# Five block-product groups per column pair in the down product, weight sums in another order, and the last gain row loaded in four pieces

## The chip, the cores and the metric

One Trainium2 chip, one core. The metric is the device time in microseconds (us); lower is better. The kernel before takes 2435.97 us, the median of three runs (2435.7 to 2436.27).

## The reference, cut to what matters

The reference is a three-layer block on 256 tokens of width 2048, in float32. The change sits in three of its linear layers, and in the last norm:

```
out = (mixed * scale * silu(g)) @ pool_w_out        # 4096 -> 2048, "pool_out"
out = (o * silu(g)) @ mla_w_out                     # 2048 -> 2048, "mla_out"
h   = h + y @ w_down                                # 5504 -> 2048, "down"
out = rms_norm(h, norm_final)                       # h * rsqrt(mean(h*h) + eps) * gain
```

`y` is the 256 x 5504 result of the gated up product. Its 5504 columns are 43 tiles of 128.

## The kernel before, in words

**Products.** A float32 product is made of three matmuls on split operands: high part times high part, high times low, low times high. Weights come from HBM in units of two 128-row tiles by 512 columns (512 KB) into a ring of 8 slots, `raw`. ScalarE writes the high part of a unit into `w_hi` (L1613, L1790), VectorE writes the low part, `w_lo = raw - w_hi` (L2443, L2451), both into rings of 4 slots, and TensorE multiplies (L963 to L965 in the layers of this change). A whole unit costs TensorE 2 tiles x 2 token halves x 3 = 12 matmuls of 512 columns. ScalarE may refill a slot once TensorE has used it (`w_used`), VectorE follows ScalarE (`w_hi`), TensorE follows VectorE (`w_lo`), and SyncE reloads a `raw` slot when the last low part that reads it is written.

**Groups.** Output columns are handled in pairs of 512-column chunks (0 and 1, then 2 and 3). For some of the tiles, a group of four units (two pairs of row tiles by two chunks, the blocks B11, B12, B21, B22) and the two token halves are multiplied with seven block products in place of eight, after Strassen. Each block product is 6 matmuls, so a group costs 42 matmuls where four whole units cost 48. In exchange the weights of a group need four sums on VectorE (L2465, L2467, L2469, L2473) and seven splits on each of ScalarE and VectorE in place of four. The sums of `y` that the groups use are made before the first group: `y_sum` (L2484 to L2492), then their high parts on ScalarE (L2365) and low parts on VectorE (L3447). Four extra PSUM banks hold what a group's blocks share; `quads_out` (L3510 to L3525) reads them into `h` once a pair's last group is done: nine VectorE instructions of 512 columns.

**Order.** `DOWN` writes out by hand the order of whole units and groups of the down product. A pair has 4 groups (tiles 24 to 39) and 14 whole units per chunk (tiles 0 to 23, 40 and 41, and tile 42 alone). In the first pair each group follows four whole units. ScalarE and VectorE walk through the same list, and after certain steps of it do other work: the high and low parts of `y` (`DOWN_Y_STEPS`, L2370 and L3450), `quads_out`, adding finished chunks into `h` (`columns_out`, L2501), squares of `h` on ScalarE (`square_out`, L1647).

**The end.** The last four whole units of chunk 3 are multiplied first for token half 0, then for half 1 (`turned_ending`). GpSimd multiplies chunks 1, 0 and 2 of `h` by the gain of the last norm (L3671), each after ScalarE has squared it. The gain row is one DMA of 1024 KB (L3589, behind the up product). VectorE waits for all three multiplications (L3551), then adds chunk 3 for half 0 (L3555), takes the reciprocal root (L3570), scales (L3573, L3575), adds chunk 3 for half 1 (L3561, L3566) and scales that. SyncE stores the results.

Of the kernel before, what the change touches and what calls it, by code (L numbers as in the profile page):

```python
# [25 lines left out]
D = 2048  # L26
# [45 lines left out]

POOL_QUADS = [20, 24, 28]
P0, P1, P2, P3 = ([("plain", c, (k, k + 1)) for k in range(0, 20, 2)] for c in range(NCH))
PQ = [[("quad", n, k)] for n, k in enumerate(POOL_QUADS)]
POOL_OUT = [P0[:9] + P1[:1] + PQ[0] + P1[1:4] + PQ[1] + P1[4:7] + PQ[2] + P1[7:] + P0[9:],
            P2[:4] + PQ[0] + P2[4:7] + PQ[1] + P2[7:9] + P3[:1] + PQ[2] + P2[9:] + P3[1:]]
# [3 lines left out]
D0, D1, D2, D3 = ([("plain", c, kts) for kts in DOWN_WHOLE] for c in range(NCH))  # L81
DOWN_ENDING = DOWN_WHOLE[-RING:]
DQ = [[("quad", n, k)] for n, k in enumerate(DOWN_QUADS)]
# [7 lines left out]
M2, M3 = ([("plain", c, (k, k + 1)) for k in range(0, 8, 2)] for c in (2, 3))  # L91
MQ = [[("quad", n, k)] for n, k in enumerate(MLA_OUT_QUADS)]
MLA_OUT = [[], M2[:3] + MQ[0] + M3[:2] + MQ[1] + M2[3:] + M3[2:]]


def quad_tables(first_unit, pairs, before):

    loads, released, quads_end, plain_end = [], [], [], {}
    last_quad = 0
    products = first_unit + before  # L100
    for p, steps in enumerate(pairs):
        for kind, c, kts in steps:
            if kind == "plain":
                loads.append((kts, c))
                released.append(products)
                products += 1
                plain_end[c] = products
            else:
                j1, j2 = (kts, kts + 1), (kts + 2, kts + 3)
                loads += [(j1, 2 * p), (j1, 2 * p + 1), (j2, 2 * p + 1), (j2, 2 * p)]  # L110
                released += [products + 3, products + 3, products + 5, products + 6]
                products += 7
                last_quad = products
        quads_end.append(last_quad)
    return loads, released, quads_end, plain_end
# [3 lines left out]
POOL_LOADS, POOL_RELEASED, POOL_QUADS_END, POOL_PLAIN_END = quad_tables(UNITS_END["pool"], POOL_OUT, 0)  # L119
SINCE_MLA_OUT = SINCE_POOL_OUT + 3 * len(MLA_OUT_QUADS)  # L120
MLA_OUT_PAIR = UNITS_END["heads"] + 16
MLA_OUT_LOADS, MLA_OUT_RELEASED, MLA_OUT_QUADS_END, MLA_OUT_PLAIN_END = quad_tables(MLA_OUT_PAIR, MLA_OUT, SINCE_POOL_OUT)
DOWN_LOADS, DOWN_RELEASED, DOWN_QUADS_END, DOWN_PLAIN_END = quad_tables(UNITS_END["up"], DOWN, SINCE_MLA_OUT)
# [8 lines left out]
assert POOL_RELEASED[-RAW:] == [UNITS_END["pool_out"] + SINCE_POOL_OUT - RAW + n for n in range(RAW)]  # L132
# [126 lines left out]
def build(nc, a, out):  # L259
# [190 lines left out]
    fgain = arena("final_gain", 0, [128, D])  # L450
    class Paired:

        def __init__(self, name, y, yh, yl, tiles, sums, sums_hi, sums_lo, quads, steps, loads, quads_end, plain_end, pairs_before):
# [3 lines left out]
            self.steps, self.loads, self.quads_end, self.plain_end, self.pairs_before = steps, loads, quads_end, plain_end, pairs_before  # L457
            self.both = len(steps[0]) > 0
# [13 lines left out]
        def blocks(self, j, tt):  # L472
# [5 lines left out]
    fsums, fsums_lo = (arena(name, 8192, [128, 3, nq, 2, 128], dt) for name, dt in (("ffn_y_sums", F32), ("ffn_y_sums_lo", F32R)))  # L478
    fsums_hi = [arena(f"ffn_y_sums_hi{n}", 8192 + (3 + n) * 1024 * nq, [128, nq, 2, 128], F32R) for n in range(3)]
# [239 lines left out]
    def _(pe):  # L719
# [238 lines left out]
        pe.wait_ge(S("ident_in"), 16)  # L958
# [8 lines left out]
        def paired(x, split, ending=()):  # L967

            def pair(p):
# [21 lines left out]
                def plain(c, kts):  # L991
# [12 lines left out]
                def block(dst, name, yh_, yl_, final=False):  # L1004

                    wh, wl = weight_slot()
                    for n in range(2):
                        cols = slice(n * 512, n * 512 + 512)
                        last = times(dst, yh_[:, n], yl_[:, n], wh[:, cols], wl[:, cols], n == 0 and begins(name), final and n == 1)
# [3 lines left out]
                def quad(q, k):  # L1013

                    e1, e5, e6, e7 = x.quad_banks(p)
                    c, last = 2 * p, q == len(x.quads) - 1
                    y_ready(k)
                    y1, y2 = slice(k, k + 2), slice(k + 2, k + 4)
                    t0, t1 = slice(0, 128), slice(128, 256)
                    block(e1, "e1", x.yh[:, y1, t0], x.yl[:, y1, t0], last)  # L1020
                    block(x.bank(c + 1, 0), (c + 1, 0), x.sums_hi[2][:, q], x.sums_lo[:, 2, q])
                    if x.both:
                        block(e5, "e5", x.yh[:, y1, t1], x.yl[:, y1, t1], last)
                    else:
                        block(e5, "e5", x.sums_hi[3][:, q], x.sums_lo[:, 3, q], last)
                    block(e7, "e7", x.sums_hi[0][:, q], x.sums_lo[:, 0, q], last)
                    block(x.bank(c, 0), (c, 0), x.yh[:, y2, t0], x.yl[:, y2, t0])
                    block(e6, "e6", x.sums_hi[1][:, q], x.sums_lo[:, 1, q], last)
                    block(x.bank(c, 1), (c, 1), x.yh[:, y2, t1], x.yl[:, y2, t1])
                    t.add("unit", 4)  # L1030
                    t.add("more", -4)
# [31 lines left out]
                final = {c: (c, kts) for kind, c, kts in x.steps[p] if kind == "plain"}  # L1063
# [8 lines left out]
                steps = x.steps[p][:-len(ending)] if p == 1 and ending else x.steps[p]  # L1072
                for kind, c, kts in steps:
                    if (kind == "quad" or c == 2 * p + 1) and begins("all sets"):
                        for s in range(2):
                            pe.wait_ge(S(f"mm_free{s}"), t.at(f"set{s}", 1))
                    if kind == "plain":
                        plain(c, kts)
                    else:
                        if c == 0 and not x.both:  # L1080
                            pe.wait_ge(S(split), len(POOL_Y) + 1)
                        elif c == 0 and p == 0:
                            pe.wait_ge(S(split), x.tiles.index("sums") + 1)
                        quad(c, kts)
# [516 lines left out]
    def _(act):  # L1601
# [191 lines left out]
        def loaded(n, cols=1024):  # L1793

            u = t.n["unit"] + n
# [3 lines left out]
        def summed(n, k):  # L1799

            act.wait_ge(S("w_sums"), t.n.get("w_sums", 0) + k)
            return raw[:, (t.n["unit"] + n) % RAW, :]

        def step_hi(kind, kts):

            if kind == "plain":
                product_hi(loaded(0, 512 * len(kts)))
                t.add("unit")
                t.add("more", -1)
            else:  # L1810
                product_hi(loaded(0))
                product_hi(loaded(2))
                product_hi(summed(0, 1))
                product_hi(summed(1, 2))
                product_hi(loaded(3))
                product_hi(summed(2, 3))
                product_hi(summed(3, 4))
                t.add("unit", 4)
                t.add("more", -4)
                t.add("w_sums", 4)  # L1820
# [86 lines left out]
        for n, (kind, _, kts) in enumerate(POOL_OUT[0]):  # L1907
            if n >= 6:
                step_hi(kind, kts)
# [10 lines left out]
        for n, (kind, _, kts) in enumerate(POOL_OUT[1]):  # L1920
            step_hi(kind, kts)
# [1776 lines left out]
```

## Time and profile before

| | us |
|---|---|
| median of 3 runs | 2435.97 |
| span of the profiled execution, first to last instruction | 2434.2 |
| TensorE busy | 2423.9 |
| VectorE busy | 1720.3 |
| ScalarE busy | 1373.7 |
| GpSimd busy | 64.7 |

The profile is of one execution. It gives its span, 2434.2 us; the device time of that same execution isn't listed, so it is the span that a sum can be made against, and the medians lie 1.8 us above it. A matmul's printed duration is its latency; matmuls are pipelined, and what one costs is the distance from its start to the next one's. The same holds, to a smaller degree, for VectorE and ScalarE.

### The profile page before, as it was taken

To read this page: it belongs to the slowest core of one execution; us is meant where nothing else is said; L and a number is where in the kernel's file an instruction comes from. 1 tells how busy PE (TensorE), PEld (TensorE's weight loads), DVE (VectorE), ACT (ScalarE), POOL (GpSimd) and SP (SyncE) were. 2 spreads that over 40 slices of the span, in tenths; PEclk is the share of its full clock that TensorE was granted. 3 is DMA by queue.
4 is the path that set the end of the run, shared out by engine and by line. 5 is a ranking of instruction groups with operands and counts; after the bars stand their busy time and mean duration, and the time that the engine had idled before them with its cause. 6 is when DMAs were issued, how large, how long until landed. Compare 5 with 4: busy or idle time off the path is not lost.

```text
span 2434.2 us, 33996 instructions
## 1 busy us (share of the span) xinstructions
PE 2423.9 (100%) x12679; PEld 2084.6 (86%) x12679; DVE 1720.3 (71%) x2083; ACT 1373.7 (56%) x1823; POOL 64.7 (3%) x79
## 2 busy tenths in 40 slices
PE   9999999999999999999999999999999999999998
PEld 8888888888889999888888888888988888888887
DVE  7675757899765656796756667665767657679887
ACT  6444444556656666565755556565644545455555
POOL 0000000001100000010000000000000000000001
PEclk9999999999999999999999999999999999999999
DMA  8666666565555554565585554454565565656654
GB/s 314 199 189 185 188 189 183 188 218 199 180 175 181 179 158 147 211 212 189 165 235 163 161 171 151 164 178 154 172 191 180 189 190 180 191 169 205 220 184 145
DMA packets 234595, 453.03 MB, mean 186 GB/s; under 512 B 14929, under 2 KB 60417, under 8 KB 233324
## 3 DMA queue, kind: packets, MB, share of 16 engines
q1 hardware_dynamic: 230960, 435.94, 55.9%
q0 software_dynamic: 3120, 14.90, 1.7%
q10 hardware_dynamic: 396, 0.59, 0.2%
q8 instruction: 75, 1.23, 0.2%
q14 instruction: 44, 0.36, 0.0%
HBM read 448.68 MB, written 2.69 MB: 185 GB/s over the span
## 4 chain that ended last, share of the span: by engine, by line
PE 99%; DVE 1%; ACT 0%; issue 0%; ACTq 0%; DVEq 0%
PE ps L813 25%; PE ps L815 13%; PE ps L779 12%; PE ps L781 12%; PE ps L780 12%; PE ps L963 6%; PE ps L964 6%; PE ps L965 6%; PE ps L737 1%; PE ps L844 1%; PE ps L846 1%; PE ps L845 1%; PE ps L1443 1%; PE ps L1214 0%; PE ps L1202 0%; PE ps L1401 0%
## 5 line engine op out<-in xcount | busy, mean ns | idle before, releaser
L2443 DVE TENSOR_TENSOR w_lo<-raw,w_hi 128x1024 fp32r<-128x1024 f32 x689 | 842.1, 1228 | 466.7 <-ACT w_hi L1613 446.8
L1613 ACT ACTIVATE w_hi<-raw 128x1024 fp32r<-128x1024 f32 x689 | 726.8, 1060 | 650.9 <-PE ps L815 357.7
L813 PE MATMUL ps<-x_hi_lo,w_hi 128*128 128x512 f32 x2336 | 821.0, 394 | 0.0
L815 PE MATMUL ps<-x_hi_lo,w_lo 128*128 128x256 f32 x2336 | 660.7, 283 | 0.0
L813 PEld LDWEIGHTS ps<-x_hi_lo,w_hi 128*128 128x128 f32 x2336 | 438.8, 188 | 101.2
L779 PE MATMUL ps<-w_hi,x_hi_lo 128*128 128x512 f32 (+3 forms) x1184 | 461.9, 390 | 0.0
L781 PE MATMUL ps<-w_hi,x_hi_lo 128*128 128x512 f32 (+3 forms) x1184 | 453.7, 383 | 0.0
L780 PE MATMUL ps<-w_lo,x_hi_lo 128*128 128x512 f32 (+3 forms) x1184 | 452.7, 382 | 0.0
L815 PEld LDWEIGHTS ps<-x_hi_lo,w_lo 128*128 128x128 f32 x2336 | 439.3, 188 | 0.0
L1790 ACT ACTIVATE w_hi<-raw 128x1024 fp32r<-128x1024 f32 (+1 forms) x201 | 209.4, 1051 | 169.8 <-PE ps L965 152.2
L2451 DVE TENSOR_TENSOR w_lo<-raw,w_hi 128x1024 fp32r<-128x1024 f32 (+1 forms) x201 | 243.2, 1228 | 35.4 <-ACT w_hi L1790 35.1
L781 PEld LDWEIGHTS ps<-w_hi,x_hi_lo 128*128 128x128 f32 x1184 | 222.5, 188 | 39.1
L779 PEld LDWEIGHTS ps<-w_hi,x_hi_lo 128*128 128x128 f32 x1184 | 222.8, 188 | 36.5 <-issue 1.2
L780 PEld LDWEIGHTS ps<-w_lo,x_hi_lo 128*128 128x128 f32 x1184 | 222.9, 188 | 35.9
L964 PE MATMUL ps<-w_lo,ffn_y_hi 128*128 128x512 f32 (+1 forms) x283 | 111.0, 392 | 0.0
L965 PE MATMUL ps<-w_hi,ffn_y_lo 128*128 128x512 f32 (+1 forms) x283 | 111.0, 392 | 0.0
L963 PE MATMUL ps<-w_hi,ffn_y_hi 128*128 128x512 f32 (+1 forms) x283 | 111.0, 392 | 0.0
L813 PE MATMUL ps<-pooled_hi_lo,w_hi 128*128 128x512 f32 x256 | 90.0, 393 | 0.0
L963 PE MATMUL ps<-w_hi,pool_y_hi 128*128 128x512 f32 x208 | 82.3, 396 | 0.0
L964 PE MATMUL ps<-w_lo,pool_y_hi 128*128 128x512 f32 x208 | 82.1, 395 | 0.0
L965 PE MATMUL ps<-w_hi,pool_y_lo 128*128 128x512 f32 x208 | 82.1, 395 | 0.0
L815 PE MATMUL ps<-pooled_hi_lo,w_lo 128*128 128x256 f32 x256 | 72.4, 283 | 0.0
(469 smaller groups left out, 2711.9 us busy)
## 6 DMA issues: line engine op xcount, KB each, us to landing
raw<-in_w_up SPq DMA_DIRECT2D x160, 512.0 KB, 3.9
raw<-in_pool_w_in SPq DMA_DIRECT2D x126, 512.0 KB, 3.8
raw<-in_w_in SPq DMA_DIRECT2D x96, 480.0 KB, 3.8
raw<-in_w_down SPq DMA_DIRECT2D x84, 512.0 KB, 5.1
raw<-in_pool_w_out SPq DMA_DIRECT2D x64, 512.0 KB, 4.8
raw<-in_ple_w_gate SPq DMA_DIRECT2D x64, 512.0 KB, 4.3
raw<-in_mla_w_in SPq DMA_DIRECT2D x56, 448.0 KB, 3.5
raw<-in_pool_w_group SPq DMA_DIRECT2D x32, 512.0 KB, 4.1
```

The source lines that it names most:

```text
L779: pe.matmul(dst, xhi[:, k, tok], wh, start=k == units[0][0], stop=False)
L780: pe.matmul(dst, xhi[:, k, tok], wl, start=False, stop=False)
L781: last = pe.matmul(dst, xlo[:, k, tok], wh, start=False, stop=k == units[-1][-1])
L813: pe.matmul(bank, w_hi[:, slot, cols], xs[:, k].rearrange("p s n -> p (s n)"), start=k == 0, stop=False, skip_group_check=True)
L815: last = pe.matmul(bank[:, 0:T], w_lo[:, slot, cols], xs[:, k, 0, :], start=False, stop=k == nkt - 1, skip_group_check=True)
L963: pe.matmul(dst, yh_, wh, start=first, stop=False)
L964: pe.matmul(dst, yh_, wl, start=False, stop=False)
L965: return pe.matmul(dst, yl_, wh, start=False, stop=final)
L1613: act.activation(w_hi[:, t.slot(), :], raw[:, slot, :], ACT.Copy).then_inc(S("w_hi"), 1)
L1790: act.activation(w_hi[:, t.slot(), 0:cols], src, ACT.Copy).then_inc(S("w_hi"), 1)
L2443: dve.tensor_tensor(w_lo[:, t.slot(), :], raw[:, u % RAW, :], w_hi[:, t.slot(), :].bitcast(F32), ALU.subtract)\
L2451: dve.tensor_tensor(w_lo[:, t.slot(), 0:cols], src, w_hi[:, t.slot(), 0:cols].bitcast(F32), ALU.subtract).then_inc(S("w_lo"), 1)
```

## The change

The down product gets five groups per pair in place of four (tiles 20 to 39), and so 12 whole units per chunk in place of 14. Groups in the first pair now follow 9, 3, 3, 3 and 2 whole units; in the second pair 4, 3, 3, 3 and 2, with nine steps behind the last group. The group's weight sums have other signs and another order (B12 + B11 first, into the slot of B12), in all three layers; there are still four, all on VectorE. The sums of `y` grow from 1024 to 1280 columns per partition, and the low parts of `y` have one more piece (tiles 20 to 23). The buffers of the sums now begin at 2048 bytes into the arena and cover part of the gain row's place, so the gain row is loaded in four pieces of 256 KB: chunk 1 where the whole row was loaded, the others after the last group. The wait on the causal mask is merged into that of the identity.

```diff
+PARTS = ("B11", "B22", "T1", "B21", "T3", "T2", "T4")
+SLOT_OF = {"B12": 0, "T1": 0, "B11": 1, "T3": 1, "B22": 2, "T2": 2, "B21": 3, "T4": 3}
+LAST_USE = ("T1", "T3", "T2", "T4")
-DOWN_QUADS = [24, 28, 32, 36]
-DOWN_WHOLE = [tuple(range(k, min(k + 2, FKT))) for k in (*range(0, 24, 2), 40, 42)]
+DOWN_QUADS = [20, 24, 28, 32, 36]
+DOWN_WHOLE = [tuple(range(k, min(k + 2, FKT))) for k in (*range(0, 20, 2), 40, 42)]
...
-DOWN = [D0[:10] + DQ[0] + D1[:4] + DQ[1] + D1[4:8] + DQ[2] + D1[8:12] + DQ[3] + D1[12:] + D0[10:],
-        D2[:4] + DQ[0] + D2[4:8] + DQ[1] + D2[8:12] + DQ[2] + D3[:4] + DQ[3] + D2[12:] + D3[4:]]
-DOWN_Y_STEPS = {6: 3, 7: 4, 11: 5, 13: 6, 17: 7, 22: 8}
-DOWN_Y = [(0, 8), (8, 16), (16, 24), (24, 28), "sums", (28, 32), (32, 36), (36, 40), (40, 43)]
+DOWN = [D0[:9] + DQ[:1] + D1[:3] + DQ[1:2] + D1[3:6] + DQ[2:3] + D1[6:9] + DQ[3:4] + D1[9:11] + DQ[4:] + D1[11:] + D0[9:],
+        D2[:4] + DQ[:1] + D2[4:7] + DQ[1:2] + D2[7:9] + D3[:1] + DQ[2:3] + D3[1:4] + DQ[3:4] + D3[4:6] + DQ[4:] + D2[9:] + D3[6:]]
+DOWN_Y_STEPS = {6: 3, 7: 4, 8: 5, 10: 6, 12: 7, 15: 8, 19: 9}
+DOWN_Y = [(0, 8), (8, 16), (16, 20), (20, 24), "sums", (24, 28), (28, 32), (32, 36), (36, 40), (40, 43)]
...
-                loads += [(j1, 2 * p), (j1, 2 * p + 1), (j2, 2 * p + 1), (j2, 2 * p)]
-                released += [products + 3, products + 3, products + 5, products + 6]
+                loads += [(j1, 2 * p + 1), (j1, 2 * p), (j2, 2 * p + 1), (j2, 2 * p)]
+                released += [at[part] for part in LAST_USE]
...
-    fgain = arena("final_gain", 0, [128, D])
+    fgain = {c: arena(f"final_gain{c}", 2048 * n, [128, 512]) for n, c in enumerate((1, 0, 2, 3))}
...
+    FSUMS = 32768 - 6 * 1024 * nq
...
@@ scalar engine @@
-            if n in (23, 26):
-                square_out((26 - n) // 3)
-            if n == 30:
+            if n in (21, 23):
+                square_out((23 - n) // 2)
+            if n == 28:
                 square_out(2)
...
@@ vector engine, one group @@
+                b12, b11, b22, b21 = (raw[:, (u + n) % RAW, :] for n in range(4))
+                product_lo(raw[:, (u + SLOT_OF[kind]) % RAW, :])
+                if kind == "B11" and by_vector:
+                    dve.wait_ge(S(f"raw_full{u % RAW}"), 16 * (u // RAW + 1))
+                    dve.tensor_tensor(b12, b12, b11, ALU.add).then_inc(S("w_added"), 16)
+                elif kind == "B22":
+                    dve.wait_ge(S("w_added"), 16 * (t.n.get("quad", 0) + 1))
+                    dve.tensor_tensor(b22, b22, b12, ALU.add).then_inc(S("w_sums"), 1)
+                elif kind == "T1":
+                    dve.wait_ge(S("w_sums"), 3 * t.n.get("quad", 0) + 1)
+                    dve.tensor_tensor(b11, b22, b11, ALU.subtract).then_inc(S("w_sums"), 1)
+                elif kind == "T3":
+                    dve.tensor_tensor(b21, b21, b22, ALU.add).then_inc(S("w_sums"), 1)
...
@@ vector engine, down product @@
-            if 28 <= n <= 28 + 3:
-                quads_out(0, n - 28)
+            if n in (27, 28):
+                quads_out(0, n - 27)
+        for n in (2, 3):
+            quads_out(0, n)
...
@@ GpSimd @@
-        load(fgain, a["norm_final_2"].unsqueeze(0).broadcast_to([128, D]), "final_gain_in")
+        def final_gain(c):
+
+            load(fgain[c], a["norm_final_2"][c * 512:c * 512 + 512].unsqueeze(0).broadcast_to([128, 512]), "final_gain_in")
+
+        final_gain(1)
+        pool.wait_ge(S("w_used"), RING + down.quads_end[1])
         pool.wait_ge(S("final_gain_in"), 16)
+        for c in (0, 2, 3):
+            final_gain(c)
         for n, c in enumerate((1, 0, 2)):
+            if n:
+                pool.wait_ge(S("final_gain_in"), 16 * NCH)
             pool.wait_ge(S("squared_out"), NCH + 3 + n + 1)
```

In the second pair, VectorE still starts `quads_out(1, ...)` at step 23 and `columns_out(down, h, 2)` at step 27. Before, the pair had 32 steps (0 to 31); now it has 29 (0 to 28).

## Rows read from the trace of the kernel before

**Rows 1.** The page: busy time of the engines.
```profile
PE 2423.9 (100%) x12679; PEld 2084.6 (86%) x12679; DVE 1720.3 (71%) x2083; ACT 1373.7 (56%) x1823; POOL 64.7 (3%) x79
```
**Rows 2.** The page: chain that ended last, by engine.
```profile
PE 99%; DVE 1%; ACT 0%; issue 0%; ACTq 0%; DVEq 0%
```
**Rows 3.** Busy time in stretches: down product's first pair, then second.
```profile
core 0: us, PE busy (x) PEld busy (x) DVE busy (x) ACT busy (x) POOL busy (x), PEclk, DMA share, GB/s
2200.00:2300.00 100.00, 100.00 (x432) 81.08 (x431) 92.14 (x82) 58.78 (x58) 0.00 (x0) 1.00 0.59 200
2300.00:2422.00 122.00, 122.00 (x527) 98.91 (x526) 103.37 (x102) 65.33 (x72) 9.23 (x6) 1.00 0.54 177
```
**Rows 4.** Timeline of PE: first and last matmul of the down product.
```profile
2197.90 0.39 PE L963 MATMUL ps<-w_hi,ffn_y_hi 128*128 128x512 f32 x1
...
2426.52 0.29 PE L965 MATMUL ps<-w_hi,ffn_y_lo 128*128 128x256 f32 x1
```
**Rows 5.** Timeline of DVE up to the end of the first group.
```profile
2202.01 1.23 DVE L2484 TENSOR_TENSOR ffn_y_sums<-ffn_y 128x1024 f32<-128x1024 f32 x1
...
2213.37 3.49 DVE L3447 TENSOR_TENSOR ffn_y_sums_lo<-ffn_y_sums,ffn_y_sums_hi 128x1024 fp32r<-128x1024 f32 x3
2216.78 3.49 DVE L2451 TENSOR_TENSOR w_lo<-raw,w_hi 128x1024 fp32r<-128x1024 f32 x3
...
2221.57 1.22 DVE L2451 TENSOR_TENSOR w_lo<-raw,w_hi 128x1024 fp32r<-128x1024 f32 x1 [0.17 <-ACT w_hi L1790]
...
2224.36 1.23 DVE L2451 TENSOR_TENSOR w_lo<-raw,w_hi 128x1024 fp32r<-128x1024 f32 x1 [0.43 <-ACT w_hi L1790]
...
2227.14 1.23 DVE L2451 TENSOR_TENSOR w_lo<-raw,w_hi 128x1024 fp32r<-128x1024 f32 x1 [0.42 <-ACT w_hi L1790]
2228.54 1.23 DVE L2451 TENSOR_TENSOR w_lo<-raw,w_hi 128x1024 fp32r<-128x1024 f32 x1 [0.17 <-ACT w_hi L1790]
...
2230.82 3.57 DVE L2451 TENSOR_TENSOR w_lo<-raw,w_hi 128x1024 fp32r<-128x1024 f32 x3
```
**Rows 6.** Timeline of ACT: a high part within a group, and its wait.
```profile
2227.44 1.06 ACT L1790 ACTIVATE w_hi<-raw 128x1024 fp32r<-128x1024 f32 x1 [0.33 <-PE ps L965]
```
**Rows 7.** Timeline of DVE behind the second pair's last group.
```profile
2398.39 0.69 DVE L3510 COPY down_sum<-ps 128x512 f32<-128x512 f32 x1
2398.99 0.68 DVE L3511 TENSOR_TENSOR h<-h,ps 128x512 f32<-128x512 f32 x1
...
2400.18 2.23 DVE L2451 TENSOR_TENSOR w_lo<-raw,w_hi 128x1024 fp32r<-128x1024 f32 x1
...
2405.88 2.32 DVE L2451 TENSOR_TENSOR w_lo<-raw,w_hi 128x1024 fp32r<-128x1024 f32 x1
...
2410.45 1.27 DVE L2501 TENSOR_TENSOR h<-h,ps 128x512 f32<-128x512 f32 x2
```
**Rows 8.** Timeline of POOL from the up product's end.
```profile
2198.36 0.54 POOL L3589 DMA_DIRECT2D final_gain<-in_norm_final  x1 [632.13 <-PE ps L815]
2398.78 2.55 POOL L3671 TENSOR_TENSOR h<-h,final_gain 128x512 f32<-128x512 f32 x2 [199.88 <-ACTq L2358]
2405.67 3.68 POOL L3671 TENSOR_TENSOR h<-h,final_gain 128x512 f32<-128x512 f32 x2 [4.34 <-ACTq L2358]
2416.83 3.00 POOL L3671 TENSOR_TENSOR h<-h,final_gain 128x512 f32<-128x512 f32 x2 [7.47 <-ACTq L2358]
```
**Rows 9.** Timeline of ACT: first square of chunk 2.
```profile
2415.24 0.61 ACT L1647 ACTIVATE junk<-h 128x512 f32<-128x512 f32 x1
```
**Rows 10.** Timeline of DVE: the closing steps.
```profile
2419.93 0.16 DVE L3551 TENSOR_REDUCE mean_square<-square_sums 128x2 f32<-128x6 f32 x1 [1.26 <-POOL h L3671]
...
2421.89 0.69 DVE L3555 TENSOR_TENSOR h<-h,ps 128x512 f32<-128x512 f32 x1 [1.60 <-PE ps L965]
...
2424.35 0.75 DVE L3575 SCALAR_TENSOR_TENSOR h<-h,rstd,final_gain 128x512 f32<-128x512 f32 x1
2425.76 0.69 DVE L3561 TENSOR_TENSOR h<-h,ps 128x512 f32<-128x512 f32 x1 [0.67 <-PE ps L965]
```
**Rows 11.** DMA issues: the gain row, KB and us to landing.
```profile
final_gain<-in_norm_final POOLq DMA_DIRECT2D x1, 1024.0 KB, 8.3
```

More of the change, by code:

```diff
@@ L86 @@
-DOWN_Y_STEPS = {6: 3, 7: 4, 11: 5, 13: 6, 17: 7, 22: 8}
-DOWN_Y = [(0, 8), (8, 16), (16, 24), (24, 28), "sums", (28, 32), (32, 36), (36, 40), (40, 43)]
-MLA_OUT_QUADS = [8, 12]
[L91 to L98, printed above, removed]
+DQ = quads_at(DOWN_QUADS)
@@ L99, in quad_tables, with paired_tables @@
+MQ = quads_at(MLA_OUT_QUADS)
+MLA_OUT = [[], M2[:3] + MQ[:1] + M3[:2] + MQ[1:] + M2[3:] + M3[2:]]
+def paired_tables(first_unit, pairs, before):
+    loads, released, quads_end, plain_end, steps, units = [], [], [], {}, [], []
     last_quad = 0
     products = first_unit + before
-    for p, steps in enumerate(pairs):
-        for kind, c, kts in steps:
+    for p, pair in enumerate(pairs):
+        steps.append([])
+        for entry in pair:
+            unit = first_unit + len(loads)
+            steps[-1].append([(kind, c, kts, unit) for kind, c, kts in entry])
+            at = {kind: products + n for n, (kind, _, _) in enumerate(entry)}
+            products += len(entry)
+            kind, c, kts = entry[0]
@@ L103, in quad_tables @@
             if kind == "plain":
                 loads.append((kts, c))
-                released.append(products)
-                products += 1
+                released.append(at[kind])
                 plain_end[c] = products
             else:
+                units.append(unit)
                 j1, j2 = (kts, kts + 1), (kts + 2, kts + 3)
-                loads += [(j1, 2 * p), (j1, 2 * p + 1), (j2, 2 * p + 1), (j2, 2 * p)]
-                released += [products + 3, products + 3, products + 5, products + 6]
@@ L112, in quad_tables @@
-                products += 7
+                loads += [(j1, 2 * p + 1), (j1, 2 * p), (j2, 2 * p + 1), (j2, 2 * p)]
+                released += [at[part] for part in LAST_USE]
                 last_quad = products
         quads_end.append(last_quad)
-    return loads, released, quads_end, plain_end
+    return loads, released, quads_end, plain_end, steps, units
 SINCE_POOL_OUT = 3 * 2 * len(POOL_QUADS)
-POOL_LOADS, POOL_RELEASED, POOL_QUADS_END, POOL_PLAIN_END = quad_tables(UNITS_END["pool"], POOL_OUT, 0)
+POOL_LOADS, POOL_RELEASED, POOL_QUADS_END, POOL_PLAIN_END, POOL_STEPS, POOL_SUMS = paired_tables(UNITS_END["pool"], POOL_OUT, 0)
@@ L1008, in block, with part @@
                         cols = slice(n * 512, n * 512 + 512)
-                        last = times(dst, yh_[:, n], yl_[:, n], wh[:, cols], wl[:, cols], n == 0 and begins(name), final and n == 1)
+                        last = times(dst, yh_[:, n], yl_[:, n], wh[:, cols], wl[:, cols], n == 0 and begins(bank), closing[bank] == i and n == 1)
                     last.then_inc(S("w_used"), 1)
                     t.add("more")
-                def quad(q, k):
+                def part(i, name, q, k):
@@ L1026, in quad @@
[L1026 to L1031, printed above, removed]
+                    if name == "B11":
+                        y_ready(k)
+                        t.add("unit", 4)
+                        t.add("more", -4)
+                        block(i, e1, "e1", x.yh[:, y1, t0], x.yl[:, y1, t0])
+                    elif name == "B22":
+                        block(i, x.bank(c + 1, 0), (c + 1, 0), x.sums_hi[2][:, q], x.sums_lo[:, 2, q])
+                    elif name == "B21":
+                        block(i, x.bank(c, 0), (c, 0), x.yh[:, y2, t0], x.yl[:, y2, t0])
+                    elif name == "T1" and x.both:
+                        block(i, e5, "e5", x.yh[:, y1, t1], x.yl[:, y1, t1])
+                    elif name == "T1":
+                        block(i, e5, "e5", x.sums_hi[3][:, q], x.sums_lo[:, 3, q])
+                    elif name == "T3":
+                        block(i, e7, "e7", x.sums_hi[0][:, q], x.sums_lo[:, 0, q])
+                    elif name == "T2":
+                        block(i, e6, "e6", x.sums_hi[1][:, q], x.sums_lo[:, 1, q])
+                    else:
+                        block(i, x.bank(c, 1), (c, 1), x.yh[:, y2, t1], x.yl[:, y2, t1])
@@ L1071, in pair @@
                     pe.wait_ge(S(f"mm_free{s}"), t.at(f"set{s}", 1))
-                steps = x.steps[p][:-len(ending)] if p == 1 and ending else x.steps[p]
-                for kind, c, kts in steps:
-                    if (kind == "quad" or c == 2 * p + 1) and begins("all sets"):
+                steps = parts[:-len(ending)] if p == 1 and ending else parts
+                for i, (kind, c, kts, _) in enumerate(steps):
+                    if (kind != "plain" or c == 2 * p + 1) and begins("all sets"):
                         for s in range(2):
@@ L1791, in product_hi, with loaded, step_hi @@
             t.add("more")
-        def loaded(n, cols=1024):
-            u = t.n["unit"] + n
+        def loaded(u, cols=1024):
             act.wait_ge(S(f"raw_full{u % RAW}"), 16 * (u // RAW + 1))
             return raw[:, u % RAW, 0:cols]
[L1799 to L1820, printed above, removed]
+        def step_hi(entry):
+            for kind, _, kts, u in entry:
+                if kind == "plain":
+                    product_hi(loaded(u, 512 * len(kts)))
+                elif kind in ("B11", "B22", "B21"):
+                    product_hi(loaded(u + SLOT_OF[kind]))
+                else:
+                    if kind == "T1":
+                        act.wait_ge(S("w_added"), 16 * (t.n.get("quad", 0) + 1))
+                    else:
+                        act.wait_ge(S("w_sums"), 3 * t.n.get("quad", 0) + {"T2": 1, "T3": 2, "T4": 3}[kind])
+                    product_hi(raw[:, (u + SLOT_OF[kind]) % RAW, :])
+            plains = entry[0][0] == "plain"
+            t.add("unit", 1 if plains else 4)
+            t.add("more", -1 if plains else -4)
+            if not plains:
+                t.add("quad")
         for g in range(WB):
@@ L3670, in _ @@
             for tt in range(2):
[L3671 removed]
+                last = pool.tensor_tensor(h[:, tt, cols], h[:, tt, cols], fgain[c], ALU.mult)
             last.then_inc(S("final_gained"), 1)
```

177 lines of the change are left out of this document (82 added, 95 removed).

## The prediction, made before the changed kernel ran

> **What bounds the kernel now.** I read the busy times first, then the chain of work that ended last, then the down product in stretches, then the timelines of its engines. TensorE is busy for 2423.9 of 2434.2 us [rows 1], and 99% of the chain is its own [rows 2]. So fewer matmuls shorten the kernel, as long as TensorE finds its operands ready. In the first pair of the down product VectorE is busy for 92 us of 100, in the second for 103 of 122 [rows 3]. The change takes matmuls away and gives VectorE work, in the place where VectorE has least room. That is the question here.
>
> TensorE doesn't pause in the down product: its starts stand about 0.23 us apart throughout. By the code it has 2 pairs x (4 groups x 42 + 2 chunks x 27 tiles x 6) = 984 matmuls of 512 columns; first start to last start is 228.6 us, with the last one's own 0.12 it is 228.74 [rows 4], so one costs 0.2325 us.
>
> **Part 1, TensorE's work.** One more group per pair saves 6 matmuls, 12 in all: 972 in place of 984, 12 x 0.2325 = -2.79 us. All of it is on the path.
>
> **Part 2, the start of the first pair.** A VectorE instruction of 1024 columns costs 1.137 us from start to start (three in 3.41 us [rows 5]), one of 512 costs 0.60 [rows 7], so 256 columns more cost 0.27 and one of 1280 costs 1.40.
>
> Where is the margin before? TensorE reaches the sixth product of the first group after 10 whole units and 5 blocks: 150 matmuls, 2197.90 + 34.87 = 2232.77. Its low part is the first of the three that begin at 2230.82, and is done at 2232.04 [rows 5]. The margin is 0.73 us, and VectorE has been at work since 2202.01 with gaps of 0.17, 0.43, 0.42 and 0.17 us, 1.19 together, in which it waited for ScalarE, and that for a free slot.
>
> After the change, until the same product: four sums of y and their three low parts are 256 columns longer, 7 x 0.27 = +1.87; the new piece of y's low part +1.14; one whole unit fewer before the group, -1.14; the gaps close, since VectorE is now the late one, -1.19. VectorE is done at 2232.04 + 0.68 = 2232.7. But the group comes one unit sooner: TensorE is there after 138 matmuls, at 2229.98. It is late by 2.7 us, and 2.8 to 3.0 with the handover; I take +2.9, spread over the products of this group.
>
> Second group: VectorE has 11 instructions for the group, 3 for whole units and 2 for y in between, 16 x 1.137 = 18.2 us; TensorE's part is 3 x 2.79 + 7 x 1.395 = 18.1. It stays late, and +0.2 is my value for it. From then on there are 15, 15 and 13 instructions per round (17.1, 16.8 with one of them of 768 columns, 14.8) against 18.1, 18.1 and 15.3 us: it catches up, and the later groups wait for nothing. The last read-outs of the pair now end some 2 us before TensorE needs the banks, 0 to +0.1. Part 2 is **+3.2 us**. The bounds are 2.7, the bare sum, and 4, if each restart of TensorE costs another 0.2.
>
> ScalarE has two more groups x 3 splits and one more piece of y; in a group it waits 0.33 us for TensorE before each split [rows 6], and 59 of 100 us are busy [rows 3]: nothing. Bytes loaded are the same. In the pool and mla layers a group has the same 11 VectorE instructions in the same pattern as before, and signs don't change a duration: nothing. The first sum now needs the group's first unit and the first product its second; loads run eight units ahead, over 20 us: nothing. The causal mask, loaded right behind the identity in the first stage, is now waited for with it, behind the whole pool product: nothing.
>
> **Part 3, the end.** Let Q be the end of the last group, E TensorE's end. Before, 22 tiles follow Q (30.7 us), now 16: E - Q = 16 x 6 x 0.2325 = 22.3 us. VectorE's read-outs still begin at step 23, but the pair ends at 28, not 31. Behind Q it has, without a pause: the product of step 23, which can begin at Q + 1.3 (ScalarE's 1.06 and two handovers [rows 6]); five products, 5.7; nine read-outs of 0.60, 5.4; two additions of chunk 2, 1.2. Alone, it is through at Q + 13.6.
>
> GpSimd now multiplies in the same stretch. Before, the products beside its multiplications took 2.23 and 2.32 us in place of 1.22 [rows 7, 8]; they had room to spare. I take that price, 2 x 1.05 = +2.1, so chunk 2 is complete at Q + 15.7 = E - 6.6. Then ScalarE's squares until GpSimd begins, 1.59 [rows 8, 9], GpSimd 3.0, to the first reduction 0.1, and about 0.4 for two tiny instructions: L3555 can begin at E - 1.5. Before, it began at E - 4.75, and had waited 1.60 us for TensorE [rows 10]. From L3555 to the end of L3575 are 3.15 us (2421.89 to 2424.35, and 0.67), so L3561 begins at E + 1.65, where it was at E - 0.88. Its last half is then no longer gated by TensorE, which gives 0.15 back. Part 3 is **+2.4 us**. Its lower bound is +0.3, with no collision at all; the upper one +5.4, if each of the four instructions in GpSimd's first two multiplications holds VectorE up for its whole 1.28 us.
>
> This bears on a rule: two rows show a product lengthened by about one GpSimd instruction [rows 7, 8]. The Trainium skill (SBUF — State Buffer, Who interferes with whom) says that a VectorE instruction with two SBUF inputs and a GpSimd instruction that reads SBUF exclude each other, and the second "fully blocks". The rows agree. By it the read-outs, which mostly have one input in PSUM, pay nothing, and the end costs between the two bounds.
>
> The three late gain pieces are issued when Q is seen, some 0.55 us each [rows 8], and land within about 8.3 us, the time of the whole row [rows 11]: by Q + 10.5. Only chunks 0, 2 and 3 wait for that, and chunk 2 is multiplied at Q + 17: nothing. Queued behind the new wait on GpSimd is chunk 1's multiplication; it starts some 2 us behind Q and delays nobody but VectorE.
>
> **Sum.** -2.79 + 3.2 + 2.4 = +2.8 us: a span of 2437.0, and with the 1.77 us between span and median 2438.8 us (+0.12%). A measurement of this kernel can tell about 0.2%, 4.9 us, from no change.
>
> **Rivals.**
> - *VectorE keeps up at the start.* Only the 2.79 us of part 1 and the 2.4 of part 3 count: 2435.6. For it: an engine's closed gaps could be more than the 1.19 I counted. Against: the margin was 0.73 us, the group comes 2.79 sooner. Chance 0.12.
> - *The end is slower: GpSimd blocks VectorE fully.* The place is the stretch behind Q; the price is +5.4 in place of +2.4: 2441.8, slower by 0.24%. It decides once the collisions cost more than 0.2 us, since that is all the room there is, and beyond it each us is one of the end. For it: the third multiplication took 3.0 and the second 3.68 us where 2.55 is the clean value [rows 8], so both sides wait. Against: five of VectorE's 16 instructions there have two SBUF inputs and are products, the read-outs between take the rest. Chance 0.13.
> - *VectorE doesn't catch up in the first pair.* If the gaps within groups (1.19 us each) don't close in groups 2 to 4, another 1 to 3 us: up to 2441.8. Chance 0.10.
> - *The matmul count doesn't fall, or another stretch changes.* The code gives 972; a wrong order would show as 984 and 2441.6. Chance 0.03.
>
> **How the numbers follow.** The forecast has 0.60, the rivals 0.38, what I haven't thought of 0.02. The range 2435.4 to 2441.6 holds the first rival, the forecast with its bounds, and half of the second and third. Slower by over 0.2% (2440.8) takes most of the second, a part of the third and of the fourth: 0.17. Faster by over 0.2% (2431.1) would need more than the whole of part 1: 0.03. Within 0.2%: 0.80.
>
> **What would show it.** In the profile after: 972 matmuls of 512 columns' worth in the down product, and a gap on TensorE of near 3 us in all at the first group of the first pair, released by VectorE's low parts, with no ACT gap before VectorE from 2202 to 2250; L3561 about 1.7 us behind TensorE's last start, waiting for nothing; two products behind Q of over 2 us. A TensorE without pauses in the first group would prove part 2 wrong; L3555 still waiting for TensorE would prove part 3 wrong.

## The result, and the profile after

The changed kernel takes 2441.01 us (median of 16 runs, 2439.82 to 2441.93), the kernel before 2435.96 us (16 runs, 2435.58 to 2436.67). The ratio is 1.0019, with a 95% interval of 1.0013 to 1.0026: slower by 5.05 us, at the edge of what the prediction counted as a difference (0.2%), and clear of the scatter. It had said 2438.8 us, in a range of 2435.4 to 2441.6.

The profiled execution is one of the faster ones, 2440.01 us with a span of 2438.2 us. Its page has these lines for busy time, the chain of work that ended last, and, among the groups, the product's first matmul (L985 now, L963 before) with its idle time and what ended it:

```profile
PE 2423.7 (99%) x12667; PEld 2080.7 (85%) x12667; DVE 1738.4 (71%) x2098; ACT 1380.4 (57%) x1830; POOL 64.7 (3%) x82
PE 95%; DVE 4%; ACT 1%; issue 0%; POOL 0%; POOLq 0%; ACTq 0%; DVEq 0%
...
L985 PE MATMUL ps<-w_hi,ffn_y_hi 128*128 128x512 f32 (+1 forms) x267 | 105.2, 394 | 1.9 <-DVE w_lo L2476 1.7
```

TensorE has 12 instructions fewer, as counted. The chain, which was TensorE's alone for 99% [rows 2], now runs through VectorE for 4%. The idle time in the row of the product's first matmul was 0.0 us and is 1.9, of which VectorE's low parts ended 1.7. In stretches of the down product (columns as in [rows 3]):

```profile
2200.00:2300.00 100.00, 98.69 (x422) 78.90 (x421) 97.93 (x85) 60.72 (x60) 0.00 (x0) 1.00 0.57 187
2300.00:2424.00 124.00, 122.97 (x526) 98.51 (x525) 116.11 (x110) 69.56 (x76) 6.72 (x7) 1.00 0.55 185
```

VectorE went from 92 to 98 us of 100 in the first pair, and from 103 of 122 to 116 of 124 in the second. The granted clock is 1.00 in both, so no part of this is TensorE's clock.

The timeline of VectorE where the first group is prepared:

```profile
2201.75 1.49 DVE L2509 TENSOR_TENSOR ffn_y_sums<-ffn_y 128x1280 f32<-128x1280 f32 x1
...
2214.52 4.29 DVE L3472 TENSOR_TENSOR ffn_y_sums_lo<-ffn_y_sums,ffn_y_sums_hi 128x1280 fp32r<-128x1280 f32 x3 [0.26 <-ACT ffn_y_sums_hi L2390]
...
2227.82 2.43 DVE L2476 TENSOR_TENSOR w_lo<-raw,w_hi 128x1024 fp32r<-128x1024 f32 x2
2230.16 1.22 DVE L2499 TENSOR_TENSOR raw<-raw 128x1024 f32<-128x1024 f32 x1
2231.30 3.57 DVE L2476 TENSOR_TENSOR w_lo<-raw,w_hi 128x1024 fp32r<-128x1024 f32 x3
```

and of TensorE at the start of the down product, at its pauses (first group, second group, handover to the second pair, last four units), and at its last matmul:

```profile
2198.49 0.39 PE L985 MATMUL ps<-w_hi,ffn_y_hi 128*128 128x512 f32 x1
...
2226.15 0.40 PE L987 MATMUL ps<-w_hi,ffn_y_sums_lo 128*128 128x512 f32 x1
2226.82 0.50 PE L985 MATMUL ps<-w_hi,ffn_y_hi 128*128 128x512 f32 x1 [0.27 <-DVE w_lo L2476]
2227.15 0.39 PE L986 MATMUL ps<-w_lo,ffn_y_hi 128*128 128x512 f32 x1
...
2229.09 0.50 PE L985 MATMUL ps<-w_hi,ffn_y_hi 128*128 128x512 f32 x1 [0.63 <-DVE w_lo L2476]
...
2232.57 0.50 PE L985 MATMUL ps<-w_hi,ffn_y_sums_hi 128*128 128x512 f32 x1 [0.42 <-DVE w_lo L2476]
...
2250.57 0.40 PE L987 MATMUL ps<-w_hi,ffn_y_sums_lo 128*128 128x512 f32 x1
2250.90 0.50 PE L985 MATMUL ps<-w_hi,ffn_y_sums_hi 128*128 128x512 f32 x1
...
2313.51 0.40 PE L987 MATMUL ps<-w_hi,ffn_y_lo 128*128 128x512 f32 x1
2314.08 0.47 PE L985 MATMUL ps<-w_hi,ffn_y_hi 128*128 128x512 f32 x1 [0.17 <-DVE w_lo L2476]
...
2420.22 0.40 PE L987 MATMUL ps<-w_hi,ffn_y_lo 128*128 128x512 f32 x1
2421.29 0.50 PE L985 MATMUL ps<-w_hi,ffn_y_hi 128*128 128x512 f32 x1 [0.66 <-DVE w_lo L2476]
...
2428.70 0.28 PE L987 MATMUL ps<-w_hi,ffn_y_lo 128*128 128x256 f32 x1
```

The bracket understates a pause, because a matmul's printed duration is its latency. Count from start to start instead: 2226.15 to 2226.82 is 0.67 us where 0.23 is usual, so 0.44 us were lost, and the next distance, 0.33, loses another 0.10. Summed this way over all distances above 0.27 us, TensorE lost 2.7 us in the first pair (2.1 of it at the first group, 0.2 at the second, 0.4 at the handover to the second pair) and 1.7 us in the last four units. That fits the ends: from first to last matmul start it was 228.62 us before [rows 4], is 230.21 now, and 228.62 - 2.79 + 4.4 = 230.2.

The end of the kernel, timelines of VectorE and of GpSimd behind the last group:

```profile
2406.47 4.03 DVE L2476 TENSOR_TENSOR w_lo<-raw,w_hi 128x1024 fp32r<-128x1024 f32 x1 [0.26 <-ACT w_hi L1820]
...
2412.22 2.01 DVE L2476 TENSOR_TENSOR w_lo<-raw,w_hi 128x1024 fp32r<-128x1024 f32 x1
...
2421.16 1.27 DVE L2526 TENSOR_TENSOR h<-h,ps 128x512 f32<-128x512 f32 x2
2422.35 0.68 DVE L2476 TENSOR_TENSOR w_lo<-raw,w_hi 128x512 fp32r<-128x512 f32 x1
2426.79 0.16 DVE L3578 TENSOR_REDUCE mean_square<-square_sums 128x2 f32<-128x6 f32 x1 [3.76 <-POOL h L3707]
...
2427.06 0.68 DVE L3582 TENSOR_TENSOR h<-h,ps 128x512 f32<-128x512 f32 x1
...
2430.17 0.68 DVE L3588 TENSOR_TENSOR h<-h,ps 128x512 f32<-128x512 f32 x1
```

```profile
2405.24 1.60 POOL L3616 DMA_DIRECT2D final_gain<-in_norm_final  x3 [205.74 <-PE ps L987]
2406.86 2.56 POOL L3707 TENSOR_TENSOR h<-h,final_gain 128x512 f32<-128x512 f32 x2
2410.58 2.56 POOL L3707 TENSOR_TENSOR h<-h,final_gain 128x512 f32<-128x512 f32 x2 [1.17 <-DMA final_gain<-in_norm_final]
2424.13 2.55 POOL L3707 TENSOR_TENSOR h<-h,final_gain 128x512 f32<-128x512 f32 x2 [10.98 <-ACTq L2383]
```

Two products took 4.03 and 2.01 us in place of 1.22: 3.6 us more, beside GpSimd's first two pairs of multiplications. L3582 (L3555 before) no longer waits for TensorE [rows 10]; it waits for GpSimd's third pair, and L3588 (L3561 before) begins 1.47 us behind TensorE's last start, where it began 0.76 us ahead of it.

The account of this execution against the one before: the down product began 0.6 us later (2198.49 against 2197.90); matmuls -2.8; pauses of the first pair +2.7; pauses at the end +1.7; from the last matmul's start to the end of the span 9.5 in place of 7.7, +1.8. Together +4.0, the difference of the spans. In the profiles of the experiments below it began between 2197.70 and 2198.73, though no edit there takes or adds a matmul ahead of it: most of the 0.6 us is scatter. The pool_out product is an example: from its first to its last matmul it took 170.26 us before, 170.87 here, in e4 and in e7, and 170.33 to 170.35 in the other five. All eight profiles of the new code share a loss of no more than 0.1 us there.

### The profile page after: what moved, and what is told of

Read it like the earlier page. It is cut to its first block, busy times and chain, and to the rows that moved or that the text cites. A ratio compares the mean times of both kernels' runs of the same rounds, so it can differ in the third digit from the quotient of the medians.

```text
span 2438.2 us, 34024 instructions
## 1 busy us (share of the span) xinstructions
PE 2423.7 (99%) x12667; PEld 2080.7 (85%) x12667; DVE 1738.4 (71%) x2098; ACT 1380.4 (57%) x1830; POOL 64.7 (3%) x82
## 3 DMA queue, kind: packets, MB, share of 16 engines
q8 instruction: 75, 1.23, 0.2%
## 4 chain that ended last, share of the span: by engine, by line
PE 95%; DVE 4%; ACT 1%; issue 0%; POOL 0%; POOLq 0%; ACTq 0%; DVEq 0%
PE ps L835 25%; PE ps L837 13%; PE ps L801 12%; PE ps L803 12%; PE ps L802 12%; PE ps L985 5%; PE ps L986 5%; PE ps L987 5%; DVE w_lo L2476 1%; PE ps L759 1%; PE ps L866 1%; PE ps L868 1%; PE ps L867 1%; PE ps L1473 1%; PE ps L1244 0%
## 5 line engine op out<-in xcount | busy, mean ns | idle before, releaser
L1820 ACT ACTIVATE w_hi<-raw 128x1024 fp32r<-128x1024 f32 (+1 forms) x207 | 215.1, 1051 | 164.6 <-PE ps L987 132.6
L2476 DVE TENSOR_TENSOR w_lo<-raw,w_hi 128x1024 fp32r<-128x1024 f32 (+1 forms) x207 | 251.4, 1232 | 21.2 <-ACT w_hi L1820 20.6
L985 PE MATMUL ps<-w_hi,ffn_y_hi 128*128 128x512 f32 (+1 forms) x267 | 105.2, 394 | 1.9 <-DVE w_lo L2476 1.7
L987 PE MATMUL ps<-w_hi,ffn_y_lo 128*128 128x512 f32 (+1 forms) x267 | 104.7, 392 | 0.0
L986 PE MATMUL ps<-w_lo,ffn_y_hi 128*128 128x512 f32 (+1 forms) x267 | 104.6, 392 | 0.0
L985 PE MATMUL ps<-w_hi,pool_y_hi 128*128 128x512 f32 x208 | 82.3, 396 | 0.1
```

What stands on the lines that cost most here:

```text
L985: pe.matmul(dst, yh_, wh, start=first, stop=False)
L986: pe.matmul(dst, yh_, wl, start=False, stop=False)
L987: return pe.matmul(dst, yl_, wh, start=False, stop=final)
L1820: act.activation(w_hi[:, t.slot(), 0:cols], src, ACT.Copy).then_inc(S("w_hi"), 1)
L2476: dve.tensor_tensor(w_lo[:, t.slot(), 0:cols], src, w_hi[:, t.slot(), 0:cols].bitcast(F32), ALU.subtract).then_inc(S("w_lo"), 1)
```

## The experiments

Each ran in five rounds beside the kernel before, whose median was 2436.29 us on both occasions. When the changed kernel was measured it was 2435.96, so a difference between medians of different occasions is uncertain by some 0.3 us. Diffs are against the changed kernel.

**e1: without the gain multiplications of chunks 1 and 0.**

```diff
+            w = 512 if c == 2 else 1
             for tt in range(2):
-                last = pool.tensor_tensor(h[:, tt, cols], h[:, tt, cols], fgain[c], ALU.mult)
+                last = pool.tensor_tensor(h[:, tt, cols][:, 0:w], h[:, tt, cols][:, 0:w], fgain[c][:, 0:w], ALU.mult)
```

> Leaves out the gain multiplications of chunks 1 and 0 on GpSimd but for one column each; all else as after the change. Theory 1 (GpSimd's multiplications hold up VectorE's products behind the last group): the two products of 4.03 and 2.01 us fall to 1.2, TensorE's pauses in the closing stretch (1.7 us in the trace after) nearly vanish, and the time falls by 3 to 3.6 us, to about 2437.6. Theory 2 (the read-outs alone are too dense there, with or without GpSimd): TensorE's pauses stay above 1 us and the time falls by less than 1 us.

Measured: 2436.26 us (2435.68 to 2437.07), ratio to before 1.0000 (0.9991 to 1.0009). VectorE's timeline at the same place, then TensorE's waits, longest first:

```profile
2405.90 1.23 DVE L2476 TENSOR_TENSOR w_lo<-raw,w_hi 128x1024 fp32r<-128x1024 f32 x1 [0.26 <-ACT w_hi L1820]
...
2408.84 1.21 DVE L2476 TENSOR_TENSOR w_lo<-raw,w_hi 128x1024 fp32r<-128x1024 f32 x1
...
2422.88 0.68 DVE L3582 TENSOR_TENSOR h<-h,ps 128x512 f32<-128x512 f32 x1
```

```profile
PE ps L976 <- DVE ones_square L2633: 2.1, 1, 2.1
PE ps L985 <- DVE w_lo L2476: 1.3, 3, 0.6
```

and GpSimd's timeline behind the last group:

```profile
2404.66 1.60 POOL L3616 DMA_DIRECT2D final_gain<-in_norm_final  x3 [205.95 <-PE ps L987]
2406.28 1.03 POOL L3708 TENSOR_TENSOR h<-h,final_gain 128x1 f32<-128x1 f32 x2
```

The products are back at 1.2 us, TensorE's pauses at the end are gone altogether, those of the first pair stay (2.7 us from start to start). GpSimd still issued its three DMAs, the last of them while the first product ran, so it is the multiplications that hold VectorE up, not the issues. Theory 1 holds, and the price is larger than the 3 to 3.6 us that it said: 4.75 us between the medians. In the profiles it is 4.1 us of span (2438.2 and 2434.1), of which 0.8 is where the down product began, which leaves 3.3; the rest of the 4.75 stays open (see below).

**e2: the groups of the second pair sooner.**

```diff
-        D2[:4] + DQ[:1] + D2[4:7] + DQ[1:2] + D2[7:9] + D3[:1] + DQ[2:3] + D3[1:4] + DQ[3:4] + D3[4:6] + DQ[4:] + D2[9:] + D3[6:]]
+        D2[:4] + DQ[:1] + D2[4:6] + DQ[1:2] + D2[6:8] + DQ[2:3] + D2[8:9] + D3[:1] + DQ[3:4] + D3[1:3] + DQ[4:] + D2[9:] + D3[3:]]
...
-            if n in (21, 23):
-                square_out((23 - n) // 2)
-            if n == 28:
+            if n in (18, 20):
+                square_out((20 - n) // 2)
+            if n == 26:
...
-            if 23 <= n <= 23 + 3:
-                quads_out(1, n - 23)
-            if n == 23 + 4:
+            if 20 <= n <= 20 + 3:
+                quads_out(1, n - 20)
+            if n == 20 + 4:
```

> In the second pair the groups follow 4, 2, 2, 2 and 2 whole units in place of 4, 3, 3, 3 and 2, and the read-outs, squares and gains begin three steps sooner; 36 us of work of 12 steps lie behind the last group in place of nine steps. GpSimd's collisions stay. Theory 1 (the end is late because what is behind the last group takes longer than TensorE's rest): the whole of part 3 goes, about 3.3 us, to 2437.7, though products still take 2 to 4 us beside GpSimd. Rival: with two whole units between groups VectorE (13 instructions, 14.8 us, against 15.3) falls behind in the second pair, TensorE pauses there, and less than 1 us is won.

(The 36 us there should read some 31: three whole units, 8.4 us, more than the 22.3 of the changed kernel.)

Measured: 2436.87 us (2435.87 to 2437.49), ratio 1.0002 (0.9993 to 1.0011). VectorE's timeline behind the last group and at the closing step:

```profile
2398.04 4.05 DVE L2476 TENSOR_TENSOR w_lo<-raw,w_hi 128x1024 fp32r<-128x1024 f32 x1 [0.26 <-ACT w_hi L1820]
...
2407.27 1.78 DVE L3545 TENSOR_TENSOR h<-h,down_sum 128x512 f32<-128x512 f32 x1
2408.98 1.78 DVE L3546 TENSOR_TENSOR h<-h,down_sum 128x512 f32<-128x512 f32 x1
...
2422.72 0.69 DVE L3582 TENSOR_TENSOR h<-h,ps 128x512 f32<-128x512 f32 x1 [0.81 <-PE ps L987]
```

The collisions are all still there, and this time two read-outs of `down_sum` pay as well (1.78 in place of 0.68 us). Yet 4.1 us are won (3.3 were expected): L3582 waits for TensorE again, and of TensorE's pauses at the end 0.4 us are left. So the collisions cost next to nothing by themselves; they cost where less room lies behind the last group than VectorE's work and its holdups take. The rival falls: no pause appears between the groups of the second pair, though only two whole units separate them.

**e3: one piece of y's low part behind the first group.**

```diff
-DOWN_Y_STEPS = {6: 3, 7: 4, 8: 5, 10: 6, 12: 7, 15: 8, 19: 9}
+DOWN_Y_STEPS = {6: 3, 7: 4, 10: 5, 11: 6, 12: 7, 15: 8, 19: 9}
```

The piece of tiles 24 to 27 goes behind the group, and the one after it moves from step 10 to 11.

> The low part of y's piece of tiles 24 to 27 moves from step 8 to step 10, behind the first group of the first pair. Theory A (what counts is VectorE's unbroken backlog up to the second group): the pauses move from the first group to the second, their sum stays at 2.7 us, time within 0.5 us of after. Theory B (only the work ahead of the first group counts): pauses fall by 1.1 us and the time by 1.1 us.

Measured: 2440.93 us (2439.78 to 2441.33), ratio 1.0018 (1.0009 to 1.0027). TensorE's restarts in the first two groups:

```profile
2230.74 0.50 PE L985 MATMUL ps<-w_hi,ffn_y_sums_hi 128*128 128x512 f32 x1 [0.43 <-DVE w_lo L2476]
...
2246.71 0.50 PE L985 MATMUL ps<-w_hi,ffn_y_hi 128*128 128x512 f32 x1 [0.38 <-DVE w_lo L2476]
...
2250.20 0.50 PE L985 MATMUL ps<-w_hi,ffn_y_sums_hi 128*128 128x512 f32 x1 [0.42 <-DVE w_lo L2476]
```

The pauses at the first group fell from 2.1 to 1.0 us, those at the second rose from 0.2 to 1.3, and the sum stayed at 2.7. Theory A holds: work moved behind one group is paid at the next, as long as VectorE's backlog has no gap between them.

**e4: the groups of the first pair later.**

```diff
-DOWN = [D0[:9] + DQ[:1] + D1[:3] + DQ[1:2] + D1[3:6] + DQ[2:3] + D1[6:9] + DQ[3:4] + D1[9:11] + DQ[4:] + D1[11:] + D0[9:],
+DOWN = [D0[:10] + DQ[:1] + D1[:3] + DQ[1:2] + D1[3:6] + DQ[2:3] + D1[6:8] + DQ[3:4] + D1[8:10] + DQ[4:] + D1[10:] + D0[10:],
...
-DOWN_Y_STEPS = {6: 3, 7: 4, 8: 5, 10: 6, 12: 7, 15: 8, 19: 9}
+DOWN_Y_STEPS = {6: 3, 7: 4, 11: 5, 12: 6, 15: 7, 17: 8, 20: 9}
```

> In the first pair the first group follows 10 whole units in place of 9, the others 3, 3, 2 and 2, and the pieces of y are split later (steps 11, 12, 15, 17, 20). The second pair is untouched. Theory A: VectorE gains 2.79 - 1.14 us on TensorE before the first group and 1.14 before the second; the pauses in the first pair fall from 2.7 to about 1.1 us, the time by 1.5 to 2.1 us, to about 2439.2. Rival: the rounds with two whole units and a piece of y make up for it (VectorE 15.9 us against 15.3), and the sum of pauses stays above 2 us.

Measured: 2438.56 us (2437.48 to 2439.08), ratio 1.0009 (1.0000 to 1.0018): 2.45 us won. The pauses of the first pair are down to 0.7 us (0.3 at the fourth group, which follows two whole units, and 0.4 at the handover); those at the end stay, 2.1 us here. Theory A holds, with somewhat more won than it said.

**e5 and e6: both edits together, and the groups of the first pair spread otherwise.** e5 has the diffs of e2 and e4. e6 has this in place of e4's:

```diff
+DOWN = [D0[:10] + DQ[:1] + D1[:3] + DQ[1:2] + D1[3:5] + DQ[2:3] + D1[5:8] + DQ[3:4] + D1[8:10] + DQ[4:] + D1[10:] + D0[10:],
...
+DOWN_Y_STEPS = {6: 3, 7: 4, 11: 5, 13: 6, 18: 7, 20: 8, 22: 9}
```

> The edits of e2 and e4 together: first pair 10, 3, 3, 2, 2 with y's pieces later, second pair 4, 2, 2, 2, 2. If the two losses are separate, their gains add up: 2441.0 - 4.1 - 2.4 = 2434.5, below the kernel before. If the losses overlap (an end that is late because the start was), no more than the larger of the two gains is seen: 2436.9.

> As e5, but the first pair is 10, 3, 2, 3, 2 with y's pieces at steps 11, 13, 18, 20, 22. By VectorE's backlog the pauses of the first pair fall by another 0.3 us: 2434.2. Rival: no difference from e5 that can be told.

Measured: e5 2434.64 us (2434.03 to 2435.55), ratio 0.9994 (0.9985 to 1.0003); e6 2434.17 us (2433.80 to 2434.88), ratio 0.9992 (0.9983 to 1.0001). The gains add up: 4.14 + 2.45 = 6.6 us were to be had, and e5 has 6.4. In TensorE's starts 0.5 us of pauses are left in e6's first pair, 0.7 in e5's. TensorE's waits in e6, longest first:

```profile
PE ps L976 <- DVE ones_square L2633: 2.1, 1, 2.1
PE ps L801 <- ACT ple_proj L1740: 0.6, 1, 0.6
PE ps L985 <- DVE w_lo L2476: 0.2, 1, 0.2
```

The first two lie in other stages and are there in the changed kernel too. e6 is 6.8 us faster than the changed kernel and 2.1 us faster than the one before. The interval of that ratio just reaches 1, though the slowest of e6's 11 runs, 2434.88, is below the fastest of the 27 runs of before beside it, 2435.60. What e6 gains on e5, 0.5 us, is less than this can tell.

**e7: four groups again, the rest of the change kept.**

```diff
-DOWN_QUADS = [20, 24, 28, 32, 36]
-DOWN_WHOLE = [tuple(range(k, min(k + 2, FKT))) for k in (*range(0, 20, 2), 40, 42)]
+DOWN_QUADS = [24, 28, 32, 36]
+DOWN_WHOLE = [tuple(range(k, min(k + 2, FKT))) for k in (*range(0, 24, 2), 40, 42)]
...
-            if n in (21, 23):
-                square_out((23 - n) // 2)
-            if n == 28:
+            if n in (23, 26):
+                square_out((26 - n) // 3)
+            if n == 30:
```

(and the orders and steps of `DOWN`, `DOWN_Y_STEPS`, `DOWN_Y` and `quads_out` of before.)

> The changed kernel with four groups per pair, in the order and with the step numbers of before; the new order of the weight sums, the gain row in four pieces and the merged wait stay. Theory: they cost nothing, since VectorE has the same eleven instructions per group: 2436.0 to 2436.6, no pauses in the down product. Rival: the new order or the late pieces cost what is missing between the sum of the prediction (+2.8) and the result (+5.0): 2438.2.

Measured: 2436.04 us (2435.77 to 2437.15), ratio 1.0000 (0.9991 to 1.0009), no distance above 0.27 us between TensorE's starts in the down product. GpSimd's timeline:

```profile
2396.87 1.59 POOL L3614 DMA_DIRECT2D final_gain<-in_norm_final  x3 [197.44 <-PE ps L987]
2399.23 2.56 POOL L3705 TENSOR_TENSOR h<-h,final_gain 128x512 f32<-128x512 f32 x2 [0.76 <-ACTq L2383]
2406.25 3.54 POOL L3705 TENSOR_TENSOR h<-h,final_gain 128x512 f32<-128x512 f32 x2 [4.47 <-ACTq L2383]
```

Neither the new order of the weight sums, nor the gain row in pieces, nor the merged wait costs anything that these times can tell. The loss comes with the fifth group and the places it was given.

## Why the prediction was right, and where it was not

**Direction and kind** were right: little change, on the slow side, by two losses that eat the 12 matmuls, one at the first pair's start and one at the end. The result lies inside the range, 2.2 us above the value. In spans, where the sum said 2437.0 and the profile shows 2438.2, the 1.2 us are -0.5 in part 2, +1.1 in part 3 and the +0.6 at the start of the down product; so two mis-sized parts partly cancel, and that is luck. The other 1.0 us is that the profiled execution is faster than the median one.

**Part 1** (-2.79) holds: x12667 for x12679, and the first-to-last distance agrees within 0.03 us once the pauses are taken off. e5 and e6 show the gain where the pauses are small.

**Part 2** (+3.2) measured 2.7: 2.1 at the first group where 2.9 was said, 0.2 at the second, as said, and 0.4 at the handover where 0 to 0.1 was said. VectorE's backlog itself came out as worked out: from its first sum to the end of the sixth product 30.7 us were said, and 30.8 were measured (2201.75 to 2232.51). What was wrong is where it begins. The sum took it from the kernel before, 4.11 us behind TensorE's first matmul; it is 3.25 us behind in all seven profiles with five groups, and 4.09 in e7. The 0.85 us come from the piece of `y` for tiles 16 to 23, which is split while the up product runs. It is now tiles 16 to 19: the sum added the new piece behind it and overlooked that this one had become shorter. ScalarE's high part of it, before and after:

```profile
2165.32 1.90 ACT L2370 ACTIVATE ffn_y_hi<-ffn_y 128x2048 fp32r<-128x2048 f32 x1
...
2165.92 1.05 ACT L2395 ACTIVATE ffn_y_hi<-ffn_y 128x1024 fp32r<-128x1024 f32 x1
```

and VectorE's next product, which waits for ScalarE:

```profile
2168.20 1.23 DVE L2443 TENSOR_TENSOR w_lo<-raw,w_hi 128x1024 fp32r<-128x1024 f32 x1 [1.52 <-ACT w_hi L1613]
...
2167.95 1.23 DVE L2468 TENSOR_TENSOR w_lo<-raw,w_hi 128x1024 fp32r<-128x1024 f32 x1 [0.67 <-ACT w_hi L1643]
```

TensorE's later start in this execution has no part in it: e1 began at 2197.70 and paused for the same 2.1 us. The method, VectorE's backlog counted instruction by instruction, was right, and e3 shows why it must be a running total. The rival in which VectorE keeps up is refuted by the pauses, and the one in which it doesn't catch up too: after the second group there is no pause until the handover. (Before, the first group of the first pair followed ten whole units and the others four, as the prediction's sum has it.)

**Part 3** (+2.4) was mis-sized: +3.5 in the profiled execution, 1.7 of pauses and 1.8 behind the last matmul, and 4.14 and 4.75 by the medians of e2 and e1. The term that was too small is the price of the two collisions, taken as 2 x 1.05 us from [rows 7]. The first cost 2.81 us, more than both GpSimd multiplications together (2.56), the second 0.79: 3.6 in place of 2.1. From the end of chunk 2's additions (2422.43) to L3582 it was 4.6 us where 5.1 were said, which gives 0.5 back. In addition the prediction said that TensorE wouldn't pause there, and it did: with 3.6 us lost, VectorE's products came too late for the last four units. The rival in which GpSimd blocks VectorE fully (2441.8, 0.24%) came closer than the forecast, by its number and, at the first pair of multiplications, by its mechanism: e1 takes the collisions away and the time is that of before. Its condition (collisions over 0.2 us decide) doesn't fit the sum beside it, in which the end costs +0.3 with no collision; in e1, without them, the end costs nothing, 7.7 us from the last matmul's start as before. "The read-outs pay nothing" held in this profile, where all nine took 0.67 or 0.68 us. It doesn't hold for the three that add `down_sum` to `h` and so read two operands in SBUF: in e2 two of them paid 1.1 us each, and they are missing from the count of five instructions with two SBUF inputs.

**What costs nothing**: e7 bears out the items that it keeps (the order of the sums, the pool and mla layers, the late pieces, the merged wait), within the scatter. For ScalarE's added work there is the profile: every wait of TensorE in the down product ended with VectorE. One thing that e7 doesn't have is GpSimd's wait of 1.17 us for the late pieces before its second pair of multiplications; what it cost or saved isn't shown. The chance of 0.17 for slower by over 0.2% was low for a case whose result is 0.19%, with the rival of the full block half at work.

**Still open:** the medians differ by 5.05 us, the two profiles by 4.0 us of span, and the changed kernel's runs spread over 2.1 us where those of before spread over 1.1. Collisions that fall otherwise from run to run would do that; e3's profile, where they took 2.81, 0.14 and 1.10 us and TensorE paused for 2.1 us at the end, points the same way. None of the slower runs has a profile, so this isn't shown.

## What to carry to other kernels

When a change takes work from the bounding engine and gives it to one that is nearly always busy in that stage (92 of 100 us here), count the second engine's instructions as a running total against the first one's arrival, group by group: here the trade paid only where the total stayed nearly ahead, and where the groups stood decided that more than how many there were. Work that leaves the stretch ahead of the count moves its start, too. Read-outs, norms and other work behind the last expensive group need their own budget, holdups by GpSimd included; three whole units more behind it made the same kind of collisions nearly free.

## What the runs showed of the hardware

A VectorE product that began 0.39 us before GpSimd's multiplication (2406.47 and 2406.86) still ended only behind both of GpSimd's back-to-back instructions and took 4.03 us, 2.81 more than alone, and so it was in all six profiles with five groups and full multiplications (4.03 to 4.05 us, GpSimd 0.38 to 0.40 us behind). It is a fixed cost of where the change put the two, not scatter. In e1 the same product began 0.38 us before a GpSimd multiplication of one column; there the product took its usual 1.23 us, and that multiplication took 0.89 us where the next took 0.18. In the kernel before, a product that met the second of a pair lost 1.0 us, and one that met the first lost 1.1 while GpSimd's second waited in turn and its pair took 3.68 us [rows 7, 8]. The Trainium skill (SBUF — State Buffer, Who interferes with whom) says that the one that issues first keeps the other out for the whole instruction. With the one column of e1 the trace agrees. With the full multiplications the record of the product starts first and it is the one kept out, and for two instructions, not one. What decides that isn't visible in the traces.
